# Attention to a memory, per 128-row tile: moving the output transposes, the scaling and the evacuation in the hand-written order of three engines

## The reference

```python
def memory_cross_attention(x, mem, w_q, w_kv, w_o):
    B, S, _ = x.shape
    M = mem.shape[1]
    q = (x @ w_q).reshape(B, S, XA_HEADS, DH)
    kv = (mem @ w_kv).reshape(B, M, 2, XA_HEADS, DH)
    k, v = kv[:, :, 0], kv[:, :, 1]
    s = jnp.einsum('bqhd,bmhd->bhqm', q, k).astype(jnp.float32) * (DH ** -0.5)
    p = jax.nn.softmax(s, axis=-1).astype(v.dtype)
    o = jnp.einsum('bhqm,bmhd->bqhd', p, v).reshape(B, S, XA_W)
    return o @ w_o

y = memory_cross_attention(x, mem, xa_w_q[l], xa_w_kv[l], xa_w_o[l])
x = layer_norm(DN_ALPHA * x + y, ln_g[l, 1], ln_b[l, 1])
y = jnp.square(jax.nn.relu(x @ mlp_w_up[l])) @ mlp_w_down[l]
```

## Time and profile before

| | us |
|---|---|
| median of three executions | 3103.3 |
| lowest, highest | 3099.31, 3105.06 |
| the profiled execution, its own time | 3102.59 |
| its span | 3100.7 |
| TensorE busy (matmuls) | 2879.8 |
| VectorE busy | 1669.5 |
| ScalarE busy | 1071.9 |
| share of the ending chain on TensorE | 53% |
| memory attention, first layer | 1711.2 to 1766.1 |
| memory attention, second layer | 2684.3 to 2742.4 |

### The profile page before, as it was taken

One profiled execution on the slowest core, in us unless ns is written; L12 is line 12 of the kernel. 1 busy time (PEld: TensorE's weight loads), 2 busy tenths in 40 slices (PEclk: granted clock), 3 DMA queues, 4 the chain that ended last, 5 costly groups with the idle time before them and its releaser, 6 DMA issues.

```text
span 3100.7 us, 39666 instructions
## 1 busy us (share of the span) xinstructions
PE 2879.8 (93%) x15492; PEld 2231.3 (72%) x15492; DVE 1669.5 (54%) x3179; ACT 1071.9 (35%) x1872; POOL 448.3 (14%) x401
## 2 busy tenths in 40 slices
PE   5889989998998898998999899999899999899998
PEld 2478864688984487475887688887566688678887
DVE  6855667754678744836236642526655423663344
ACT  3333335124136521635222431322454322332231
POOL 3200013321005420402020000000222111000000
PEclk8999999999999999999999999999899999899999
DMA  5433320232233043021323223233111323123231
GB/s 172 150 127 103 102 75 1 82 96 94 69 91 55 26 117 92 1 62 55 100 97 111 81 99 104 91 99 86 49 43 35 91 99 103 55 95 104 88 107 69
DMA packets 224928, 261.75 MB, mean 84 GB/s; under 512 B 12818, under 2 KB 187010, under 8 KB 224616
## 3 DMA queue, kind: packets, MB, share of 16 engines
q1 hardware_dynamic: 207328, 203.93, 21.5%
q0 software_dynamic: 12544, 45.08, 4.2%
q10 hardware_dynamic: 4872, 10.21, 1.5%
HBM read 245.04 MB, written 13.11 MB: 83 GB/s over the span
## 4 chain that ended last, share of the span: by engine, by line
PE 53%; DVE 8%; issue 1%; ACT 1%; DMA 1%; POOL 1%; SPq 0%; DVEq 0%; ACTq 0%; POOLq 0%
PE PS L349 30%; PE PS L3718 10%; PE PS L156 3%; PE PS L3617 2%; PE PS L1182 2%; PE PS L1171 2%; PE PS L1158 2%; DVE S L1209 1%; DVE HL L297 1%; DVE S L2603 1%; DVE S L2599 1%; DVE S L1237 1%; PE PS L2443 1%; DMA S<-in_w_in 1%; ACT HL L290 1%
## 5 line engine op out<-in xcount | busy, mean ns | idle before, releaser
L349 PE MATMUL PS<-xT,HL 128*128 128x512 f32 (+1 forms) x3552 | 792.1, 384 | 15.2 <-DVE HL L297 7.1
L297 DVE TENSOR_TENSOR HL<-S,HL 128x2048 fp32r<-128x2048 f32 (+2 forms) x204 | 423.7, 2082 | 645.5 <-ACT HL L290 645.4
L349 PEld LDWEIGHTS PS<-xT,HL 128*128 128x128 f32 x3552 | 643.8, 187 | 156.9 <-DVE HL L297 8.6
L290 ACT ACTIVATE HL<-S 128x2048 fp32r<-128x2048 f32 (+2 forms) x204 | 351.5, 1729 | 674.6 <-PE PS L349 290.3
L3718 PE MATMUL PS<-HL,hd 128*128 128x512 f32 x1536 | 350.0, 389 | 0.1
L3718 PEld LDWEIGHTS PS<-HL,hd 128*128 128x128 f32 x1536 | 288.0, 188 | 60.7 <-PE PS L3718 1.0
L1268 ACT ACTIVATE S<-S,S 128x256 f32<-128x256 f32 (+5 forms) x292 | 189.2, 648 | 184.7 <-DVE S L1209 177.3
L1303 POOL TENSOR_SCALAR S<-S,S 128x512 f32<-128x512 f32 (+4 forms) x104 | 179.9, 1730 | 388.7 <-DVE S L1224 229.2
L1171 PEld LDWEIGHTS PS<-S,S 128*128 128x128 f32 (+1 forms) x1048 | 112.6, 140 | 144.0 <-issue 40.8
L1171 PE MATMUL PS<-S,S 128*128 128x128 f32 (+1 forms) x1048 | 168.4, 287 | 44.1 <-DVE S L1237 12.9
L349 PE MATMUL PS<-h_high,HL 128*128 128x512 f32 (+1 forms) x768 | 201.2, 348 | 0.1
(11 more groups left out here) (406 smaller groups left out, 3859.8 us busy)
## 6 DMA issues: line engine op xcount, KB each, us to landing
S<-in_mlp_w_up SPq DMA_DIRECT2D x32, 1024.0 KB, 5.4
S<-in_mlp_w_down SPq DMA_DIRECT2D x32, 1024.0 KB, 5.0
S<-in_w_in SPq DMA_DIRECT2D x28, 1024.0 KB, 5.3
S<-in_w_ada SPq DMA_DIRECT2D x24, 1024.0 KB, 5.2
S<-in_w_gate SPq DMA_DIRECT2D x24, 1024.0 KB, 5.1
S<-in_w_in SPq DMA_DIRECT2D x36, 512.0 KB, 5.2
S<-in_w_mix_out SPq DMA_DIRECT2D x8, 1024.0 KB, 5.1
spectra<-S POOLq DMA_DIRECT2D x24, 256.0 KB, 4.8
```

The costliest lines, as they stand in the source:

```text
L290: m = a.activation(high, raw, ACT.Copy)
L297: m = v.tensor_tensor(low, raw, high.bitcast(F32), ALU.subtract)
L349: m = pe.matmul(dst, l[x], r[y], start=(i == 0 and j == 0), stop=(i == n - 1 and j == 2))
```

## The change

Three moves inside the loop over the tiles, with the semaphore numbering moved along; no instruction is added or taken away, and every one keeps its waits.

- TensorE: values(t+1) go ahead of products(t); out(t+1) stays behind products(t), so the products now stand between the two.
- VectorE: scaling(t+1) goes from behind variance(t) to ahead of sums(t).
- ScalarE: copy out(t+1) goes from behind root(t) to ahead of it.

The turn of the outputs of tile t-1 stays behind out(t+1). What is ahead of the loop (the whole of tile 0's attention, tile 1's scores) keeps its order.

```diff
@@ residual: plan
             if ahead:
                 ahead.plan_outer(t)
             var[t], root[t] = dv.next(), ac.next()
-            if ahead:
-                ahead.plan_last(t)
             ready[t] = [dv.next(), dv.next()]
@@ residual: dve
                 dve_variance(t)
-                if ahead:
-                    ahead.dve_outer(t)
                 dve_norm(t)
@@ residual: act
                 act_root(t)
-                if ahead:
-                    ahead.act_outer(t)
                 if t - 1 in turns:
@@ MemoryTiles
         def plan_values(self, t):
             self.free["values", t] = psum_free[4]
-            self.valued[t], self.out[t] = mm.next(), mm.next()
+            self.valued[t], self.scaled[t] = mm.next(), dv.next()
 
         def plan_out(self, t):
-            self.scaled[t], self.ready[t] = dv.next(), ac.next()
+            self.out[t], self.ready[t] = mm.next(), ac.next()
             psum_free[4] = self.ready[t]
@@ plan_inner
             if t < 2:
                 self.plan_scores(t + 2)
-
-        def plan_outer(self, t):
             if t < 3:
                 self.plan_values(t + 1)
 
-        def plan_last(self, t):
+        def plan_outer(self, t):
             if t < 3:
                 self.plan_out(t + 1)
@@ tensor_inner, tensor_outer
             if t < 2:
                 self.tensor_scores(t + 2)
+            if t < 3:
+                self.tensor_values(t + 1)
 
         def tensor_outer(self, t):
             if t < 3:
-                self.tensor_values(t + 1)
                 self.tensor_out(t + 1)
@@ dve
             if t < 2:
                 self.dve_low(t + 2)
-
-        def dve_outer(self, t):
             if t < 3:
                 self.dve_scale(t + 1)
@@ act
             if t < 2:
                 self.act_exp(t + 2)
-
-        def act_outer(self, t):
             if t < 3:
                 self.act_out(t + 1)
```

## The result

The changed kernel took 3108.76 us (median of 13 executions, 3104.64 to 3114.13), the kernel before 3100.2 us (median of 13, 3091.48 to 3121.89). The ratio is 1.0029 with a 95% interval of [1.0017, 1.004], 5 to 12 us slower. The forecast was 3107.0 and +3.7 us, the range 3099.5 to 3112. The direction and the time hold; the size of the step is 9 us, not 3.7.

What follows compares the result with a forecast made beforehand. Six TensorE idles of 1.22 us, where out waits for VectorE's scaling, bounded the gain at 7.3 us. New waits made the layers 1.8 and 1.9 late, clock net nothing: +3.7 us, 3107.0 us, range 3099.5 to 3112.

Steps and rivals of the forecast that it cites:

- The new waits: TensorE in each layer: values(2) and values(3) wait 0.7 and 2.0 us for copies, products(3)'s second half 3.1 for its bank.
- full-clock periods: Changed loop, from one tile's products' end to the next's, at granted clock 1.00: 8.37, 9.46 and 7.97 us.
- Tile 0: Values(1) ahead of products(0) make those end late: 1733.74 against 1732.22 (1.52) in layer one, 2706.98 against 2705.37 in layer two.
- 1.54 of low-clock excess: Kernel before, tile 3's last turn and products: 1.54 us taken off as low clock, so products(3) end at 1757.72.
- sum of +3.7 at one clock: Both layers' loops with equal low stretches: products(3) end 1.8 and 1.9 us late, together +3.7 us.
- The term of the clock: Six loop periods: four low stretches of 1.55 us charged, one per idle of 2.0 and 3.1, as many as before.
- the list of unknowns: Number of low stretches left open at 0 to 8: six waits, and one at each layer's start.
- the slower rival: Idles of 2.0 and 3.1 and the later start bring more low stretches; seven give +8.4 us, 3111.7; chance 0.15.
- the sign of the prediction that missed: Profile sign at the start of each layer's loop: products(0) end about 1.5 us later than before.
- the clock is the loss: Rival: low stretches after idles of 2.0 and 3.1 and the later start, seven making +8.4 us, 3111.7; chance 0.15.
- The table switch: ScalarE's load ahead of each root: 1.28 us, just hidden; rival of 1.82 gives +5.4 us, 3108.7, chance 0.07.
- VectorE: Early scaling hides narrowly, 0.3 us ahead in tile 1; chain from products(2) to the freed bank, 6.14, bounds the last period.

Runs made afterwards that it cites:

- the filled pair: The kernel before and the changed kernel, each with unread matmuls in the waits ahead of and in the loop: 0.9961 and 0.9977 against the kernel before.
- fill_all_before: Kernel before with unread matmuls in the waits ahead of the loop and in its waits for the scaling: 0.9961, median 3088.02 us.
- tile0_old: Changed kernel with the three moves taken back for the first pass of the loop alone: 1.0029 against the kernel before.
- after_again: The changed kernel's order unaltered, one more profiled execution, without a timing of its own.
- fill_wait: Changed kernel with unread matmuls ahead of values(3) and ahead of the second half of products(3): 1.0011 against the kernel before.
- before_again: The order of the kernel before unaltered, one more profiled execution, without a timing of its own.
- tile0_new: Kernel before with the three moves made for the first pass of the loop alone: 1.0000 against the kernel before.

## Why the prediction was right, and too small

**The new waits: right.** The forecast named them, in order and place: values(2) and values(3) on ScalarE's copies (0.7 and 2.0; measured 1.1 and 2.2), the second half of products(3) on the bank (3.1; 3.4). The full-clock periods were forecast at 8.37, 9.46 and 7.97 and are 8.68, 9.65 and 8.15. The kernel before was taken at 8.96, 8.70 and 7.84.

**Tile 0: right at one clock.** 1.52 and 1.61 late forecast; 5.4 against 3.6, 1.8 late, measured in the filled pair.

**One size hidden in the right sum.** The last period before is 8.69 at full clock, not 7.84. I took the whole 1.54 of low-clock excess in its turn and products as lost time, but the second half of products(3) waits for its bank in the kernel before too. `fill_all_before` shows the row,

```profile
PE PS L156 <- DVE xT L2455: 0.7, 1, 0.7
```

and its last half of products is released at 1746.58 by the low part. The slow clock filled that wait. So only 0.68 of the 1.54 was clock, and the change shortens the last period by 0.5. This error of 0.85 was made up by periods one to three of the changed kernel, each 0.2 to 0.3 longer than forecast, and by tile 0. That the sum of +3.7 at one clock agrees so well with the measured 3.8 is in this part luck.

**The clock: the step that failed.** The term of the clock was nothing net; it is some 5 us by the timing (9 less 3.8). I charged four stretches of 1.55 to the changed kernel, one behind each idle of 2.0 and 3.1 us, the same number that I had counted before, so that they cancelled. Four things went otherwise. Behind the idle of 1.1, which I charged nothing, there was a stretch in the first layer of both profiles (10.4 for 8.7). Behind the idle of 2.2 there was a stretch every time (1.7). Behind that of 3.4 there was none in period three, 8.15 in both profiles of the changed order. And the largest item of the first profile, the late rise at the start (3.9 and 2.6), I named in the list of unknowns and in the slower rival and priced at nothing. It is also the sign of the prediction that missed: products(0) ended 5.0 and 3.6 later than before, not 1.5. How much of the 9 us the start has on average isn't shown: it came in five layers of ten, and `tile0_old` gave it back and gained nothing. With the stages of both profiles of each order, 121.2 us against 110.4 for the two layers, the difference is 10.8; 3.8 of it is order, so 7.0 clock. The rival "the clock is the loss" gave +8.4 and 3111.7 and was nearer in size, with 0.15 where it deserved more; its mechanism held for the idle of 2.2 and in part for the start, not for the idle of 3.4. One profile of before was also too thin a base: it had four low stretches in the loops where the second has one.

**The table switch: right.** It was 1.28 and hidden. The Trainium skill, "ScalarE: Activation LUTs", section "What ACT_TABLE_LOAD costs", adds about 1.38 us of drain to each switch. The trace does not agree: the load starts 0.02 behind the copy out, the root 0.45 behind the load's end, and that gap is the wait for the variance. **VectorE**, at first sight close to being the bound, held up in the changed kernel nothing but the bank of the last period, beside the variance that each root waits for.

**What stays open.** When the late rise comes is only in part settled. In six first layers scores(2) end at the same +16.7: in the three with the values first (changed, `after_again`, `fill_wait`) the start takes 9.3 to 9.4, in the three with the products first (`before`, `before_again`, `tile0_old`) 4.2 to 4.3. So the order matters, but where scores(2) end sooner or later the changed queue shows no late rise in five layers of seven. What ahead of the stage sets this was not tried. It also isn't settled how often an untouched execution has each stretch, since a profile is one execution.

## What to carry to other kernels

A wait that is moved from one releaser to another is priced by what stands ahead of the new releaser in its own queue: here the copy, the root and a copy of a turn on ScalarE, which had been hidden under the products until the values were moved ahead of them. In a stage with pauses of one to three microseconds TensorE's clock is part of the bill: count in more than one profile how often a pause has a low stretch behind it (here, in two profiles of each order, one of 2.2 us every time in four, one of 1.2 five times in twelve, one of 3.4 never in its own period), and take a filled pair of kernels to separate order from clock. Unread matmuls in waits that can't be removed were worth more here (0.39%) than any reordering that was tried.

## What the runs showed of the hardware that was not expected

TensorE stayed at the low level (0.50, 1.2 GHz) while it was busy without a pause. The changed kernel, first layer:

```profile
1717.00:1721.00 4.00, 3.66 (x16) 3.16 (x18) 0.28 (x1) 1.47 (x3) 0.00 (x0) 0.50 0.00 0
1721.00:1723.00 2.00, 2.00 (x10) 1.35 (x9) 1.21 (x2) 0.00 (x0) 0.00 (x0) 0.50 0.00 0
1723.00:1725.00 2.00, 2.00 (x12) 2.00 (x11) 0.10 (x2) 1.93 (x8) 0.00 (x0) 0.50 0.00 0
1725.00:1727.00 2.00, 2.00 (x5) 0.97 (x5) 0.42 (x1) 0.00 (x0) 0.00 (x0) 0.50 0.00 0
1727.00:1729.00 2.00, 2.00 (x4) 0.97 (x3) 0.10 (x1) 0.00 (x0) 0.00 (x0) 0.50 0.00 0
1729.00:1731.00 2.00, 2.00 (x5) 0.72 (x4) 0.59 (x1) 0.00 (x0) 0.00 (x0) 0.82 0.00 0
```

From out(0) at 1717.34 on there was no idle time, and the level of 2.4 GHz came only behind 1729, 12 us later, through the 64-column values and most of the products. In the kernel before, with the products ahead of the values, it came 5.5 us behind out(0) (1723.50 to about 1729). The order alone does not fix it. `tile0_new` has the changed queue up to products(0), its out(0) at 1719.98, and the rise 5 us later, as values(1) begin:

```profile
1723.30:1725.30 2.00, 2.00 (x12) 1.32 (x9) 0.86 (x1) 0.20 (x1) 0.00 (x0) 0.60 0.00 0
1725.30:1727.30 2.00, 2.00 (x14) 1.56 (x14) 0.87 (x3) 1.60 (x7) 0.00 (x0) 1.00 0.00 0
```

The Trainium skill, "TensorE: Matmul & The Clock Gate", section "What's actually happening", says that the clock follows how busy TensorE has been recently. The rows of the changed kernel show a share of 1.00 for 8 us at the low level, so from the busy share of this profile the rise could not be dated.
